# First sample attention of a hybrid decoder step: which engine copies the turned keys out of PSUM

## The reference, cut to what matters

```python
def dilated_window_sample(q, k, v, buf_k, buf_v, bias_tab):
    kc = jnp.concatenate([buf_k.astype(k.dtype), k], axis=1)
    vc = jnp.concatenate([buf_v.astype(v.dtype), v], axis=1)
    ...
        logit = jnp.einsum('nthe,ntjhe->nthj', q, kg).astype(F32) + bias.astype(F32)
        ...
        p = jnp.exp(logit - mx[..., None])
        stats.append((mx, jnp.sum(p, axis=-1), jnp.einsum('nthj,ntjhe->nthe', p, vg.astype(F32))))
```

## Time and profile before

| what | us |
|---|---|
| median of three runs | 3196.35 |
| lowest, highest | 3193.88, 3202.97 |
| the profiled execution, its own time | 3219.45 |
| its span, first to last instruction | 3217.6 |
| mean granted TensorE clock in it | 0.909 |
| TensorE matmul busy | 2764.2 (86%) |
| VectorE busy | 1158.0 (36%) |
| ScalarE busy | 657.0 (20%) |
| first sample attention, from its first load at 1480.53 to the issue of its last store at 1656.43 | 175.9 |

### The profile page before, as it was taken

One profiled execution on the slowest core, in us unless ns is written; L12 is line 12 of the kernel. 1 busy time (PEld: TensorE's weight loads), 2 busy tenths in 40 slices (PEclk: granted clock), 3 DMA queues, 4 the chain that ended last, 5 costly groups with the idle time before them and its releaser, 6 DMA issues. The chain is left out here.

```text
span 3217.6 us, 34020 instructions
## 1 busy us (share of the span) xinstructions
PE 2764.2 (86%) x13628; PEld 1743.3 (54%) x13628; DVE 1158.0 (36%) x2094; ACT 657.0 (20%) x1307; POOL 366.8 (11%) x352
## 2 busy tenths in 40 slices
PE   7999999493788886885546858999999999999998
PEld 3444444142567776453324524466666666888843
DVE  0047898265666664584713402200000000000033
ACT  1122221141344443673102300100000000000011
POOL 1000000102434331000014440000000000000000
PEclk9999999685799998897767978999999999999999
DMA  6111110422144524404477684311110111110100
GB/s 231 53 40 48 38 37 31 144 55 79 30 154 124 172 73 140 144 28 142 170 225 276 243 300 166 104 64 39 39 39 26 39 39 44 63 56 15 38 33 32
DMA packets 170804, 306.84 MB, mean 95 GB/s; under 512 B 48537, under 2 KB 121961, under 8 KB 168379
## 3 DMA queue, kind: packets, MB, share of 16 engines
q1 hardware_dynamic: 145666, 176.85, 17.6%
q0 software_dynamic: 23136, 93.01, 8.2%
q10 hardware_dynamic: 1864, 35.08, 3.1%
HBM read 262.76 MB, written 69.27 MB: 103 GB/s over the span
## 5 line engine op out<-in xcount | busy, mean ns | idle before, releaser
L870 PE MATMUL m_B<-m_big,m_wdB 128*128 128x363 f32 (+1 forms) x2112 | 646.1, 468 | 3.2 <-issue 3.2
L870 PEld LDWEIGHTS m_B<-m_big,m_wdB 128*128 128x128 f32 x2112 | 400.5, 190 | 248.0 <-issue 4.9
L345 PE MATMUL i_psM<-i_w,i_xnT 128*128 128x477 f32 x1152 | 475.3, 573 | 2.3 <-ACT i_xnT L210 2.3
L345 PEld LDWEIGHTS i_psM<-i_w,i_xnT 128*128 128x128 f32 x1152 | 221.0, 194 | 246.3 <-issue 243.5
L732 DVE TENSOR_TENSOR m_actT<-m_wdB,m_B 128x363 f32 (+3 forms) x66 | 35.2, 533 | 604.1 <-PE m_B L870 604.1
L624 ACT ACTIVATE m_wdB<-m_B 128x363 f32<-128x363 f32 (+1 forms) x66 | 31.2, 473 | 599.0 <-PE m_B L870 599.0
L912 PE MATMUL m_B<-m_wdA,m_actT 128*128 128x256 f32 x704 | 152.4, 379 | 0.8 <-DVE m_actT L732 0.8
L912 PE MATMUL m_B<-m_wdB,m_actT 128*128 128x256 f32 x704 | 152.6, 379 | 0.0
L912 PEld LDWEIGHTS m_B<-m_wdA,m_actT 128*128 128x128 f32 x704 | 133.7, 190 | 19.5 <-DVE m_actT L732 1.4
L912 PEld LDWEIGHTS m_B<-m_wdB,m_actT 128*128 128x128 f32 x704 | 133.5, 190 | 18.8 <-issue 0.8
L590 POOL TENSOR_TENSOR m_rstd<-m_ms,m_half 128x1 f32<-128x1 f32 x18 | 9.9, 551 | 1133.5 <-DVE m_ms L700 1133.5
(11 more groups left out here) (405 smaller groups left out, 3676.9 us busy)
## 6 DMA issues: line engine op xcount, KB each, us to landing
proj<-i_stage SPq DMA_DIRECT2D x72, 238.5 KB, 2.8
b_Kp<-b_k SPq DMA_DIRECT2D x32, 512.0 KB, 9.0
b_Vp<-b_v SPq DMA_DIRECT2D x32, 512.0 KB, 9.0
o_bk<-b_k ACTq DMA_DIRECT2D x8, 2040.0 KB
o_bv<-b_v ACTq DMA_DIRECT2D x8, 2040.0 KB
i_w<-w_in POOLq DMA_DIRECT2D x8, 1908.0 KB, 22.8
m_wdB<-w_gate SPq DMA_DIRECT2D x22, 512.0 KB, 4.1
m_wdB<-w_up SPq DMA_DIRECT2D x22, 512.0 KB, 5.2
```

What stands on the lines that cost most here:

```text
L345: mm = nc.tensor.matmul(psM[:, c % 2, 0:CHW], xnT[:, t % 2, k, :], w[:, k, c * CHW:(c + 1) * CHW], start=(k == 0), stop=(k == KO - 1))
L870: mm = nc.tensor.matmul(B[:, bank, 0:r1 - r0], wgu[:, i, u, k, :], hnT[:, k, r0:r1], start=(k == 0), stop=(k == KO - 1))
```

## The change

In the first sample attention ScalarE does both halves of `evac_keys`, in the order of the banks; VectorE does none. In the second one (`sparse`) nothing differs: ScalarE half 0, VectorE half 1. No wait, buffer, semaphore, load or transpose is altered otherwise.

```diff
@@ ScalarE
                 for ch in range(CH):
                     for n in range(4):
-                        evac_keys(4 * ch + n, 0)
+                        for i in range(1 if sparse else 2):
+                            evac_keys(4 * ch + n, i)
                     if ch == NCH + 1:
                         softmax(0)
                 softmax(1)
@@ VectorE
                 for ch in range(CH):
                     g, c = ch // NCH, ch % NCH
-                    for n in range(4):
-                        evac_keys(4 * ch + n, 1)
+                    if sparse:
+                        for n in range(4):
+                            evac_keys(4 * ch + n, 1)
                     if ch == 0:
                         dve.wait_ge(S["bias_in"], 16 * 4 * DEC)
                     if ch:
```

## The result

The changed kernel took 3161.67 us (median of four runs, 3159.41 to 3166.51) beside 3195.11 of the kernel before in the same comparison: ratio 0.9893, 95% interval 0.9871 to 0.9915. A second comparison with more runs of before gave 3158.59 beside 3196.89: 0.9883, 0.9867 to 0.9900, which is 32 to 43 us less. The forecast was 3153.0 us, within 3145 to 3166, and 43.4 us less. The sign, the stage and the mechanism came as forecast; the gain, 33.4 and 38.3 us, was some 5 to 10 us smaller.

What follows compares the result with a forecast made beforehand. In the first sample attention, VectorE's logits and steps alternated with copies, transposes and products instead of overlapping. 44.9 - 1.0 - 0.5 = 43.4 us off the median 3196.35 gave 3153.0 us, range 3145 to 3166.

Steps and rivals of the forecast that it cites:

- 44.9 us of copies and waits go from VectorE's chain: First sample attention: without 18.7 us of copies and 11.6 and 14.6 of waits, 58.4 of 103.3 us remain.
- Bias rows 0.5 us later: Start of the stage: last bias rows share DMA engines with earlier loads, costing 0.5 us, between 0 and 4.39.
- ScalarE and its cover: ScalarE's eight copies per chunk, at most 4.8 us, cost nothing beside VectorE's 7.7 us of work.
- A tie; I put 1.0 us of waiting, between 0 and 4: VectorE's wait for products after key 19: ready between 1540 and 1542.5, wanted at 1541.6.
- key 19 lands at 1537: Key loads behind value pieces: 10.2 MB remaining at 1512, at 408 GB/s, take 25 us.
- TensorE waiting for logits instead of copies: Sign in the profile after that would show the forecast right; no size given.
- The sum: Whole gain: 44.9 - 1.0 - 0.5 = 43.4 us less, the tail's 41.7 us taken as unchanged.
- Loads at 352 GB/s: Rival: slower loads in the dense stage, key 19 at 1541, total 3155 to 3157 us; chance 0.05.
- TensorE at its low clock: Rival: TensorE stays slow, 11.0 us per chunk, and is the bound; total 3170 us; chance 0.06.
- Loads as the pace of everything: Rival: loads, not copies, set the stretch's pace at 162 GB/s; no change, 3196 us; chance 0.03.
- ScalarE as the bound: Rival: slower copies, 2.0 us each, make a chunk take 16 us; total 3214 us; chance 0.02.
- The rule weighed against it: Loads from HBM to SBUF bound at about 358 GB/s: key 19 about 3.5 us later, estimate 3156.

Runs made afterwards that it cites:

- steps late: The kernel before, VectorE still copying half of the turned keys, with all 15 selection steps behind the last logits: 3187.14 us (one execution).
- keys first: The changed kernel with all 32 key pieces issued ahead of the value pieces: 3156.07 us beside 3158.59 of the changed kernel.
- copy twice: The changed kernel with ScalarE copying each odd bank a second time into a scratch tile, 96 copies instead of 64: 3155.06 us.

## Why the prediction was right, and where it was off

- **What bounds the kernel: right.** The alternation of the earlier trace rows was the cost: it is gone after the change, and in *steps late* with VectorE still copying.
- **44.9 us of copies and waits go from VectorE's chain: right.** From its first step at 1518.04 to the softmax at 1580.47 are 62.4 us, which is the 58.4 that were to remain and the 4.0 of the new wait. In the second profiles the same 58.4 us remain (from 1512.22 to 1574.94, less a wait of 4.3), and in *keys first*, where the wait is gone, it is 58.8 us (1509.82 to 1568.62). What was removed is less certain: the second profile of before has 101.7 us from the first step to the softmax, 1.6 less than the 103.3 of the sum, so 43.3 us went instead of 44.9.
- **Bias rows 0.5 us later: not borne out.** The first pair of profiles agrees: VectorE's first step starts 31.77 us after the first load (1518.04 - 1486.27), in before 31.22 (1511.75 - 1480.53), so 0.55 later. The second pair has it the other way, 31.10 us in after (1512.22 - 1481.12) and 31.75 in before (1510.92 - 1479.17). So the rows come 31.1 to 31.8 us after the first load in either kernel, and the agreement of the first pair is luck.
- **ScalarE and its cover: right.** Eight copies in a row took 4.03 us, below the 4.8 of the prediction, and even 12 per chunk did not lengthen the stretch.
- **"A tie; I put 1.0 us of waiting, between 0 and 4": the term that was mis-sized.** It was 4.0 us in the first profile and 4.3 in the second, at and just above the upper end. The rate was right (406 to 409 GB/s against 408), and the mechanism, values between the keys, is shown by *keys first*. What failed is the step "key 19 lands at 1537", which takes a piece as in once the bytes issued up to it have been moved. Two stretches of after, from the first key load to 1517.75 and on to the turning of key 16:

```profile
1486.24:1517.75 31.51, 13.31 (x84) 11.44 (x84) 1.25 (x6) 8.37 (x16) 0.52 (x1) 0.58 0.86 251
1517.75:1544.30 26.55, 11.73 (x101) 7.77 (x97) 24.84 (x55) 8.26 (x16) 0.00 (x0) 0.79 1.03 406
```

  Key 16 came when the DMA engines had moved 18.7 MB (31.51 us x 251 GB/s and 26.55 us x 406). Everything issued up to it is 1.4 + 29 x 0.524 = 16.6 MB. So it was in 2.1 MB, about four pieces or 5 us at 406 GB/s, later than this counting has it. Counted from the first load, the prediction's 1537 for key 19 is 1542.7 in this profile (5.74 us later), and at that time not even key 16 was in. So TensorE had four pieces of the chunk to turn after its wait and not only the last one, and the products were ready at 1551.2 instead of between 1545.7 and 1548.2. The four took 5.02 us, 1.3 more than the 3.71 of the next chunk at the higher clock. Whether that 1.3 us counted is not shown: at 406 GB/s a piece of 0.524 MB takes 1.3 us, about as long as a piece took to turn here (5.02 / 4), so the loads may have set this pace as well. For the same reason, the sign "TensorE waiting for logits instead of copies" came only in part: 7.2 us for logits, 14.8 for key loads.
- **The sum.** With what the first profiles measured, 44.9 - 0.55 - 4.0 = 40.35 us in the stretch; it shrank by 40.3 (134.5 - 94.2), and by 39.6 in the second (133.4 - 93.8). The rest of the stage took 44.2 and 44.2 us before, 45.4 and 44.3 after: unchanged within its own scatter, as taken. That leaves the 39 us of the stage. So of the 4.4 us between 43.4 and 39, 3 are the wait for products, and the rest lies within what two profiles of one kernel differ by. The first comparison gives 33 us, with an interval from 27 to 41.
- **The rivals.** Loads at 352 GB/s: no, up to the arrival of key 16 they ran at 406 and were late for another reason. TensorE at its low clock: after the start only for the one chunk after the long wait. Loads as the pace of everything: no, the stretch fell by 40 us with the same loads. ScalarE as the bound: no, *copy twice* excludes it with numbers.
- **The rule weighed against it.** The loads again ran above the 358 GB/s that the Trainium skill ("DMA: Bandwidth & Descriptors", "Where 436 GB/s comes from") gives as the bound of one core's loads: 406 GB/s over 26.55 us in after. The measurement decides.

## What to carry to other kernels

Where two engines share a job and one of them has long work in the same queue, look at what the other engines wait for behind that work: the copies cost 0.7 us each, but stood behind 6.7 us of steps. Once such a circle is opened, add up by when each load must be in and compare with the order in which loads are issued, since a load order that was good enough for the slow loop can be the next limit. Then move slack work of the freed engine into its remaining waits; here two edits that gained 4 us or less each gained, together with steps that were moved forward, about 20 us. The steps were not moved alone, so the share of each is open.

## What was not expected of the hardware

Loads of 512 KB that are issued one behind the other on one queue came in later than the bytes issued up to them were moved, while the DMA engines were full: key 16 only after about 2.1 MB, four pieces, more (18.7 - 16.6). Two pieces of chunk 2 in the same trace, keys 10 and 11, show it as well, since TensorE waited for each:

```profile
1520.32 1.09 PE L2780 MATMUL b_B<-b_ident,b_Kp 128*128 128x128 f32 x8 [0.38 <-DMA b_Kp<-b_k]
...
1522.31 1.09 PE L2780 MATMUL b_B<-b_ident,b_Kp 128*128 128x128 f32 x8 [0.90 <-DMA b_Kp<-b_k]
```

From the first key load to 1520.31 are 34.07 us at 262 GB/s, 8.9 MB; issued up to key 10 are 1.4 + 11 x 0.524 = 7.2 MB. For key 11 it is 36.07 us at 268 GB/s, 9.7 MB, against 7.7. So the pieces came one by one, 2.0 us apart, and each 1.7 to 2.1 MB late. The shortest time from issue to landing of a key piece in this trace is 4.0 us, while 0.524 MB at 406 GB/s are 1.3 us; by this estimate up to 2.7 of the 5 us are there for a single load too. What makes up the rest is not shown by any run.

A copy of ScalarE that the profile shows with 0.60 us costs 0.50 in a row of eight (4.03 / 8), as the two in a row had suggested. The Trainium skill, page "Perfetto Trace Analysis", section "Optimizing Scalar/DVE Operations", says that part of an instruction's profiled time overlaps with the next one; these rows agree.
